# Expert blocks: tokens split once into high and low parts, permutation and gates as two single-pass products each

## The chip, the cores and the metric

The kernel runs on one core of a Trainium2 chip. The metric is the device time of one execution in microseconds (us). One execution was taken by the hardware profiler; every row shown below is from that one. The engines are called PE (matrix products), PEld (loads of the stationary operand of a product, which overlap PE), DVE, ACT and POOL (elementwise work) and SP (here it issues the transfers of weights).

## The reference

Two layers are computed for 384 tokens of width 1024 (128 context tokens, 256 latent ones), the first with attention, the second with a scan. Each layer ends with a grouped mixture of experts, and only that part is touched:

```python
def grouped_moe(h, router_w, router_bias, w_in, w_out, sh_in, sh_out):
    t = h.reshape(-1, d)
    scores = jax.nn.sigmoid((t @ router_w).astype(jnp.float32))
    ...
    gates = jnp.sum(jax.nn.one_hot(idx, N_EXPERTS, dtype=jnp.float32) * w[..., None], axis=1)
    hid = swiglu(jnp.einsum('td,edf->tef', t, w_in))
    routed = jnp.einsum('tef,efd->td', hid * gates[..., None].astype(hid.dtype), w_out)
    shared = swiglu(t @ sh_in) @ sh_out
    return (routed + shared).reshape(bsz, n, d)
```

There are 16 experts in 4 groups; a token goes to two experts of one group, so at most one group of four experts has gates other than zero for it.

## The kernel before

Activations lie feature by token (`hn`, 8 chunks of 128 features by 384 tokens). Products that need more than single-pass accuracy come in two kinds. One is plain fp32, one call for one product. The other, `mm3`, splits both operands into a high part of type F32R (a product of two F32R operands takes a single pass) and a low part, and makes three single-pass products, high by high, high by low and low by high (lines 1836 to 1838).

The mixture of experts is the function `moe`, written once for each engine, and runs once in each layer:

1. The router's product (line 2062), then six transposes of `hn` into token-by-feature order, jobs tok0 to tok5 (line 2077). ACT copies each from its PSUM bank to `h_tok` (line 894), and that copy gives the bank back. Six banks rotate over all jobs, so tok5 needs the bank that tok0 had, and the shared expert's first job the bank of tok1.
2. DVE finds group, experts and gates (`top_experts`, some 40 small steps, each waiting for the one before). After `member_ready` PE counts the tokens of each group (rank, line 2111), and DVE works out where each token goes (`find_places`): `place` (line 1536) is a matrix of zeros and ones, 384 tokens by 7 blocks of 128 slots. Tokens of one group are put into blocks of their own; there are 3 to 6 blocks, and in this execution 5 in the first layer and 4 in the second.
3. Meanwhile PE does the shared expert (`shared_up`, line 2088; its second matrix, line 2128).
4. `permute` (line 2097) gathers one block's tokens: for each of 8 chunks and 3 token tiles one plain product with 128x128 of `h_tok` stationary and 128 columns of `place` moving. It comes in two halves of 12 products. Block 0 is gathered ahead of the loop, both halves in a row.
5. The gates of all blocks (line 2135): 21 plain products with 128x128 of `place` stationary and 4 columns of `rt` moving.
6. The loop over blocks. Four experts each: `up` (32 products by 512 columns through `mm3`), a transpose of the hidden values (line 2162), `down` (line 2166). Weights come in 24 pieces of 512 KB to a block, through six slots: SP loads a piece into `raw`, ACT makes its high part `whi` (line 912), DVE or POOL its low part `wlo` (lines 1567, 610), PE uses them. The two halves of the next block's `permute` stand in the order between the third and fourth transposes and `down(2)` and `down(3)`, which wait for DVE's `ht_lo` (line 1579). ACT and DVE split the gathered block into `blk_hi` and `blk_lo` (lines 904, 905, 1558).
7. `place` is transposed (line 2201), and the blocks' results go back to the tokens (line 2212).

The order on each engine is written out by hand; engines wait for each other by semaphores.

Of the kernel before, what the change touches and what calls it, by code (L numbers as in the profile page):

```python
# [23 lines left out]
F32 = mybir.dt.float32  # L24
F32R = mybir.dt.float32r
ALU = mybir.AluOpType
# [3 lines left out]
P = 128  # L30
D = 1024
# [238 lines left out]
def build(nc, inp, out):  # L270
    ctx = ExitStack()
    with ctx:
# [80 lines left out]
        place = mm.put("place", [TILES, BLOCK_COLS * P])  # L353
# [3 lines left out]
        h_tok = mm.put("h_tok", [TILES, D])  # L357
# [4 lines left out]
        gates = mm.put("gates", [BLOCK_COLS, PER_GRP])  # L362
        gate_now = mm.put("gate_now", [PER_GRP])
        score_rows = mm.put("score_rows", [NTOK])
        sg = mm.put("sg", [2, NTOK])
        p2 = mm.put("p2", [2, NTOK])
# [51 lines left out]
        def sem(name):  # L418
            return ctx.enter_context(nc.semaphore(name))
# [19 lines left out]
        member_ready, groups_ready, place_ready, kmoe_in, gain_ready = (  # L439
            sem("member_ready"), sem("groups_ready"), sem("place_ready"), sem("kmoe_in"), sem("gain_ready"))  # L440
# [86 lines left out]
        def bk(job):  # L527
            return bank[BANK_OF[job][0]]

        def took(ins, job):  # L530
            ins.then_inc(bank_taken[BANK_OF[job][0]], 1)
# [137 lines left out]
        def _(act):  # L669
# [206 lines left out]
            def moe(layer, x_jobs):  # L876
# [10 lines left out]
                for i in range(2 * TILES):  # L887
                    if i == 2:
                        n = JOB[f"scores{layer}"]
                        finished(act, n)  # L890
                        took(act.copy(rt[:, 0, :], bk(n)[:, 0:TILES * NEXP]), n)
                    n = JOB[f"tok{layer}_{i}"]
                    finished(act, n)
                    took(act.copy(h_tok[:, i // 2, (i % 2) * 512:(i % 2 + 1) * 512], bk(n)[:, :]), n)
# [280 lines left out]
        def _(dve):  # L1175
# [258 lines left out]

            def top_experts(layer):
# [4 lines left out]
                def col(i, w=E):  # L1440
                    return rt[:, i, 0:w]
# [34 lines left out]
                dve.tensor_scalar(col(11, G), col(6, G), 1.0, None, ALU.mult).then_inc(member_ready, 1)  # L1476

# [3 lines left out]
                for one in (8, 9):  # L1481
# [7 lines left out]
                    if one == 8:  # L1489
# [8 lines left out]
                                     rt[:, 10, :].rearrange("p (t g i) -> p t i g", g=NGRP, i=PER_GRP), AX.X, ALU.add))  # L1498

# [39 lines left out]
            def moe(layer):  # L1539
# [3 lines left out]
                for kc in range(KC):  # L1543
                    scaled_x(kc)
                top_experts(layer)
# [280 lines left out]
        def _(pe):  # L1826
# [229 lines left out]
            def moe(layer):  # L2056
# [36 lines left out]
                def permute(it, half, base=PERM_BANK):  # L2093

                    for kc in range(4 * half, 4 * half + 4):
                        for t in range(TILES):
                            ins = pe.matmul(bank[base + kc // 4][:, (kc % 4) * P:(kc % 4 + 1) * P],  # L2097
                                            h_tok[:, t, kc * P:(kc + 1) * P], place[:, t, bass.ds(it * P, P)],
                                            start=t == 0, stop=t == TILES - 1)
                    ins.then_inc(ls.perm_done, 1)  # L2100
# [32 lines left out]
                for b_ in range(BLOCK_COLS):  # L2133
                    for t in range(TILES):
                        ins = pe.matmul(dst[:, b_ * PER_GRP:(b_ + 1) * PER_GRP], place[:, t, b_ * P:(b_ + 1) * P],
                                        rt[:, 12, t * PER_GRP:(t + 1) * PER_GRP], start=t == 0, stop=t == TILES - 1)
# [61 lines left out]
                for b_ in range(MAX_BLOCKS):  # L2198
                    dst = opened(JOB[f"back{layer}_{b_}"])
                    for t in range(TILES):  # L2200
                        ins = pe.transpose(dst[:, t * P:(t + 1) * P], place[:, t, b_ * P:(b_ + 1) * P], k("ident"))
                    ins.then_inc(jobs_done, 1)
# [356 lines left out]
```

## Time and profile before

| | us |
|---|---|
| median of 3 runs | 1413.44 |
| lowest and highest run | 1408.8 and 1415.91 |
| the profiled execution, own time | 1415.64 |
| its span, first to last instruction | 1413.8 |
| PE busy, share of the span | 1186.6, 84% |
| DVE busy, share of the span | 861.0, 61% |
| ACT busy, POOL busy | 621.8, 512.3 |
| mean granted TensorE clock | 0.923 |

The profiled execution lies 2.2 us above the median, within the spread of the three runs; 1.8 us of its time lie outside the span. Busy shares are averages over stages with different limits, so the stages of the mixture of experts are read one by one in the rows further down: the routing stage (380 to 441 us in the first layer, 1158 to 1222 us in the second) and the block loop (442 to 655 us and 1225 to 1392 us). A matmul's own duration holds its way through the array; how fast a row of them goes is read from their starts.

### The profile page before, as it was taken

To read this page: it belongs to the slowest core of one execution; us is meant where nothing else is said; L and a number is where in the kernel's file an instruction comes from. 1 tells how busy PE (TensorE), PEld (TensorE's weight loads), DVE (VectorE), ACT (ScalarE), POOL (GpSimd) and SP (SyncE) were. 2 spreads that over 40 slices of the span, in tenths; PEclk is the share of its full clock that TensorE was granted. 3 is DMA by queue.
4 is the path that set the end of the run, shared out by engine and by line. 5 is a ranking of instruction groups with operands and counts; after the bars stand their busy time and mean duration, and the time that the engine had idled before them with its cause. 6 is when DMAs were issued, how large, how long until landed. Compare 5 with 4: busy or idle time off the path is not lost.

```text
span 1413.8 us, 17268 instructions
## 1 busy us (share of the span) xinstructions
PE 1186.6 (84%) x6208; PEld 937.1 (66%) x6208; DVE 861.0 (61%) x1269; ACT 621.8 (44%) x984; POOL 512.3 (36%) x224
## 2 busy tenths in 40 slices
PE   4799877777899999999789999554548789999998
PEld 1685442336767777788589999443436776777778
DVE  2546883355336878883477700999995123588883
ACT  2524113263325657765464433423334313466661
POOL 0513120003004445554035553556553600355550
PEclk9799799996999999999999999677779999899999
DMA  8644138870225888884123333434420302589871
GB/s 336 233 149 148 60 109 334 353 264 31 91 102 179 287 299 300 290 293 170 63 81 119 118 127 106 131 115 125 119 68 1 149 0 81 173 296 324 303 265 45
DMA packets 80031, 241.68 MB, mean 171 GB/s; under 512 B 6624, under 2 KB 38880, under 8 KB 67168
## 3 DMA queue, kind: packets, MB, share of 16 engines
q1 hardware_dynamic: 46512, 218.65, 42.7%
q10 hardware_dynamic: 33456, 22.20, 5.6%
q8 instruction: 38, 0.62, 0.2%
q14 instruction: 25, 0.20, 0.0%
HBM read 236.36 MB, written 4.46 MB: 170 GB/s over the span
## 4 chain that ended last, share of the span: by engine, by line
PE 51%; DVE 19%; issue 11%; DMA 7%; POOL 5%; ACT 5%; SPq 0%; ACTq 0%; DVEq 0%; POOLq 0%
PE bank L1836 10%; PE bank L1838 9%; PE bank L1837 9%; DMA raw<-stream 4%; DVE wlo L1567 3%; PE bank L2088 3%; DVE seg L1773 3%; DMA raw<-experts 3%; POOL wlo L610 3%; PE bank L1854 3%; PE bank L2097 2%; DVE seg L1799 2%; PE bank L2212 2%; POOL wlo L593 2%; PE bank L1898 2%
## 5 line engine op out<-in xcount | busy, mean ns | idle before, releaser
L593 POOL TENSOR_TENSOR wlo<-raw,whi 128x2048 fp32r<-128x2048 f32 x42 | 192.1, 4579 | 379.4 <-ACT whi L676 379.4
L1567 DVE TENSOR_TENSOR wlo<-raw,whi 128x1024 fp32r<-128x1024 f32 x144 | 258.3, 1817 | 33.3 <-ACT whi L912 32.0
L912 ACT CAST whi<-raw 128x1024 fp32r<-128x1024 f32 x216 | 225.2, 1051 | 95.6 <-PE bank L1838 51.1
L610 POOL TENSOR_TENSOR wlo<-raw,whi 128x1024 fp32r<-128x1024 f32 x72 | 199.7, 2774 | 173.6 <-ACT whi L912 173.6
L1836 PE MATMUL bank<-hhi,whi 128*128 128x384 f32 (+1 forms) x504 | 176.4, 350 | 17.4 <-DVE hlo L1233 7.9
L1837 PE MATMUL bank<-hlo,whi 128*128 128x384 f32 (+1 forms) x504 | 173.8, 345 | 0.0
L1838 PE MATMUL bank<-hhi,wlo 128*128 128x384 f32 (+1 forms) x504 | 173.4, 344 | 0.0
L1836 PE MATMUL bank<-whi,blk_hi 128*128 128x512 f32 x288 | 116.6, 405 | 2.6 <-issue 1.4
L1836 PEld LDWEIGHTS bank<-hhi,whi 128*128 128x128 f32 (+1 forms) x504 | 96.4, 191 | 27.5 <-POOL wlo L593 11.9
L1837 PE MATMUL bank<-wlo,blk_hi 128*128 128x512 f32 x288 | 114.1, 396 | 0.0
L1838 PE MATMUL bank<-whi,blk_lo 128*128 128x512 f32 x288 | 114.1, 396 | 0.0
L1431 DVE SCALAR_TENSOR_TENSOR x<-bank,mod,x 128x128 f32<-128x128 f32 x96 | 34.5, 413 | 122.5 <-PE bank L1838 90.9
L676 ACT CAST whi<-raw 128x2048 fp32r<-128x2048 f32 x42 | 79.3, 1905 | 57.3 <-PE bank L1838 34.4
L1838 PEld LDWEIGHTS bank<-hhi,wlo 128*128 128x128 f32 (+1 forms) x504 | 96.4, 191 | 0.5
L1837 PEld LDWEIGHTS bank<-hlo,whi 128*128 128x128 f32 (+1 forms) x504 | 96.6, 192 | 0.1
L1854 PE MATMUL bank<-raw,silc 128*32 128x512 f32 x384 | 57.2, 695 | 37.6 <-DMA raw<-stream 25.0
L2330 PE MATMUL bank<-seg,xdt 128*64 128x128 f32 x384 | 38.5, 338 | 53.6 <-DVE seg L1799 43.7
L1836 PE MATMUL bank<-whi,ht_hi 128*128 128x512 f32 x144 | 59.9, 416 | 17.6 <-DVE ht_lo L1579 17.6
L2330 PEld LDWEIGHTS bank<-seg,xdt 128*64 128x64 f32 x384 | 29.2, 173 | 62.1 <-issue 62.1
L1773 DVE TENSOR_SCALAR seg<-rowb,dts 128x128 f32<-128x128 f32 x192 | 69.4, 432 | 0.1
L1127 ACT ACTIVATE seg<-seg 128x512 f32<-128x512 f32 x48 | 29.6, 626 | 82.7 <-DVE seg L1773 82.7
L1836 PEld LDWEIGHTS bank<-whi,blk_hi 128*128 128x128 f32 x288 | 55.2, 192 | 15.2 <-issue 4.2
(332 smaller groups left out, 2344.2 us busy)
## 6 DMA issues: line engine op xcount, KB each, us to landing
raw<-experts SPq DMA_DIRECT2D x216, 512.0 KB, 4.7
raw<-stream SPq DMA_DIRECT2D x93, 1024.0 KB, 6.2
rowb<-acs_rows ACTq DMA_DIRECT2D x48, 256.0 KB, 4.6
shared<-shared SPq DMA_DIRECT2D x6, 1024.0 KB, 7.9
s<-s0T ACTq DMA_DIRECT2D x8, 256.0 KB, 4.9
new_s<-pf ACTq DMA_DIRECT2D x16, 128.0 KB, 2.1
x<-xT ACTq DMA_DIRECT2D x1, 1536.0 KB, 13.6
yT<-x SPq DMA_DIRECT2D x8, 192.0 KB, 1.9
```

Source lines behind the costliest of these rows:

```text
L593: pool.tensor_tensor(wlo[:, q % SPL, :], raw[:, pos % RAW, :], whi[:, q % SPL, :].bitcast(F32), ALU.subtract).then_inc(lo_done, 1)
L610: pool.tensor_tensor(unit(wlo, j), unit(raw, j), unit(whi, j).bitcast(F32), ALU.subtract).then_inc(ls.e_lo[j % SLOTS], 1)
L676: act.copy(whi[:, q % SPL, :], raw[:, pos % RAW, :]).then_inc(hi_done, 1)
L912: act.copy(unit(whi, j), unit(raw, j)).then_inc(ls.e_hi, 1)
L1567: dve.tensor_tensor(unit(wlo, j), unit(raw, j), unit(whi, j).bitcast(F32), ALU.subtract).then_inc(ls.e_lo[j % SLOTS], 1)
L1773: ins = dve.tensor_scalar(seg[:, n % 2, dr, i * P:(i + 1) * P], rowb[:, n % 2, dr, i * P:(i + 1) * P], acs3[:, t, h:h + 1], 0.0, ALU.subtr ...
L1836: pe.matmul(dst, whi_, xhi_, start=first, stop=False)
L1837: pe.matmul(dst, whi_, xlo_, start=False, stop=False)
L1838: return pe.matmul(dst, wlo_, xhi_, start=False, stop=last)
L1854: ins = pe.matmul(bank[MOD_BANK][32 * grp:32 * grp + 32, :], silc[:, m_, :], raw[:, pos % RAW, grp * 512:(grp + 1) * 512], start=m_ == 0, ...
L2088: ins = pe.matmul(dst, w[:, c, kc, :], hn[:, kc, :], start=kc == 0, stop=kc == KC - 1)
L2330: ins = pe.matmul(dst[64 * p_:64 * p_ + 64, c * P:(c + 1) * P], lhs, rhs, start=j < 2, stop=j >= len(terms) - 2, skip_group_check=True)
```

## The change

`h_tok` is replaced by `tok_hi` and `tok_lo`, both F32R, `place` becomes F32R (zeros and ones, so it loses nothing), and each plain product of the permutation becomes two single-pass products, of `tok_hi` and of `tok_lo`, into the same sum. The gates are split in the same way into `gsplit`, and each plain product of the gates becomes two.

ACT's six copies to `h_tok` become six casts to `tok_hi`, in the same places. DVE gets six subtractions to `tok_lo` in each layer: two ahead of `top_experts`, four behind `member_ready`; these now give the banks of tok0 to tok5 back. DVE also gets two small instructions behind the gates, for `gsplit`. Some tiles are laid out anew. POOL and SP have the same rows as before.

```diff
@@ act, moe
-                    took(act.copy(h_tok[:, i // 2, (i % 2) * 512:(i % 2 + 1) * 512], bk(n)[:, :]), n)
+                    act.copy(tok_hi[:, i // 2, (i % 2) * 512:(i % 2 + 1) * 512], bk(n)[:, :]).then_inc(tok_hi_ready, 1)
@@ dve
+            def token_low(layer, i):
+
+                n = JOB[f"tok{layer}_{i}"]
+                w = slice((i % 2) * 512, (i % 2 + 1) * 512)
+                dve.wait_ge(tok_hi_ready, 2 * TILES * layer + i + 1)
+                took(dve.tensor_tensor(tok_lo[:, i // 2, w], bk(n)[:, :], tok_hi[:, i // 2, w].bitcast(F32),
+                                       ALU.subtract), n)
...
                 dve.tensor_scalar(col(11, G), col(6, G), 1.0, None, ALU.mult).then_inc(member_ready, 1)
+                for i in range(2, 2 * TILES):
+                    token_low(layer, i)
...
+                g12 = rt[:, 12, 0:TILES * PER_GRP]
+                do(dve.tensor_copy(gsplit[:, 0, :], g12))
+                do(dve.tensor_tensor(gsplit[:, 1, :], g12, gsplit[:, 0, :].bitcast(F32), ALU.subtract))
...
+                token_low(layer, 0)
+                token_low(layer, 1)
                 top_experts(layer)
@@ pe, permute
-                            ins = pe.matmul(bank[base + kc // 4][:, (kc % 4) * P:(kc % 4 + 1) * P],
-                                            h_tok[:, t, kc * P:(kc + 1) * P], place[:, t, bass.ds(it * P, P)],
-                                            start=t == 0, stop=t == TILES - 1)
+                            for part in (tok_hi, tok_lo):
+                                ins = pe.matmul(bank[base + kc // 4][:, (kc % 4) * P:(kc % 4 + 1) * P],
+                                                part[:, t, kc * P:(kc + 1) * P], place[:, t, bass.ds(it * P, P)],
+                                                start=t == 0 and part is tok_hi,
+                                                stop=t == TILES - 1 and part is tok_lo)
@@ pe, gates
-                        ins = pe.matmul(dst[:, b_ * PER_GRP:(b_ + 1) * PER_GRP], place[:, t, b_ * P:(b_ + 1) * P],
-                                        rt[:, 12, t * PER_GRP:(t + 1) * PER_GRP], start=t == 0, stop=t == TILES - 1)
+                        for i in range(2):
+                            ins = pe.matmul(dst[:, b_ * PER_GRP:(b_ + 1) * PER_GRP], place[:, t, b_ * P:(b_ + 1) * P],
+                                            gsplit[:, i, t * PER_GRP:(t + 1) * PER_GRP],
+                                            start=t == 0 and i == 0, stop=t == TILES - 1 and i == 1)
```

Two places show it in the engines' order. A row of these lists is one call of the kernel; one plain product is one row there and two instructions on the chip, as the trace's counts show (24 plain products of a block's permutation are 48 instructions).

PE in the first layer, from the shared expert to the permutation of block 0, before:

```order
L2088 MATMUL bank<-hn,shared 128x384 [waits bank_taken1,shared_in1]
L2088 MATMUL bank<-hn,shared 128x384 x7
L2088 MATMUL bank<-hn,shared 128x384 [waits bank_taken2]
L2088 MATMUL bank<-hn,shared 128x384 x7
L2097 MATMUL bank<-place,h_tok 128x128 [waits bank_taken3,place_ready]
L2097 MATMUL bank<-place,h_tok 128x128 x23
L2128 MATMUL bank<-p_105,shared 128x384 [waits shared_in2,bank_taken3,bank_taken2,bank_taken5]
```

and after:

```order
L2107 MATMUL bank<-hn,shared 128x384 [waits bank_taken1,shared_in1]
L2107 MATMUL bank<-hn,shared 128x384 x7
L2107 MATMUL bank<-hn,shared 128x384 [waits bank_taken2]
L2107 MATMUL bank<-hn,shared 128x384 x7
L2117 MATMUL bank<-place,tok_hi 128x128 [waits bank_taken3,place_ready]
L2117 MATMUL bank<-place,tok_lo 128x128
...
L2149 MATMUL bank<-p_107,shared 128x384 [waits shared_in2,bank_taken3,bank_taken2,bank_taken5]
```

The 24 calls of one permutation become 48, alternating between the two parts, at the same place and behind the same waits; in the loop, too, a half stands where it stood.

DVE in the first layer, from the scaled activations to `member_ready` (line 1476 before) and on, before:

```order
L1218 TENSOR_TENSOR hn<-x,rstd 128x384 x7
L1454 TENSOR_TENSOR rt<-rt,vec 128x48 [waits bank_taken5]
...
L1475 TENSOR_TENSOR rt<-rt 128x12 [waits dve_step]
L1476 TENSOR_SCALAR rt<-rt 128x12 [waits dve_step]
L1478 TENSOR_TENSOR rt<-rt 128x48
...
L1497 TENSOR_REDUCE rt<-rt 128x12 [waits dve_step]
L1508 COPY nums<-bank 128x16 [waits jobs_done,dve_step]
```

and after:

```order
L1222 TENSOR_TENSOR hn<-x,rstd 128x384 x7
L1444 TENSOR_TENSOR tok_lo<-bank,tok_hi 128x512 [waits tok_hi_ready] x2
L1466 TENSOR_TENSOR rt<-rt,vec 128x48 [waits bank_taken5]
...
L1487 TENSOR_TENSOR rt<-rt 128x12 [waits dve_step]
L1488 TENSOR_SCALAR rt<-rt 128x12 [waits dve_step]
L1444 TENSOR_TENSOR tok_lo<-bank,tok_hi 128x512 [waits tok_hi_ready] x4
L1492 TENSOR_TENSOR rt<-rt 128x48
...
L1511 TENSOR_REDUCE rt<-rt 128x12 [waits dve_step]
L1514 CAST gsplit<-rt 128x12 [waits dve_step]
L1515 TENSOR_TENSOR gsplit<-rt,gsplit 128x12 [waits dve_step]
L1525 COPY nums<-bank 128x16 [waits jobs_done,dve_step]
```

Two subtractions stand ahead of the routing, four behind `member_ready`, and the two instructions for `gsplit` ahead of the copy that waits for PE's rank.

## Rows read from the trace of the kernel before

**Rows 1.** PE groups by line and shape: count | busy us, mean ns | idle before.

```profile
L2097 PE MATMUL bank<-place,h_tok 128*128 x432 | 51.2, 275 | 0.0
...
L2135 PE MATMUL bank<-rt,place 128*128 128x4 f32 x84 | 11.6, 275 | 0.0
...
L2097 PE MATMUL bank<-place,h_tok 128*128 128x128 f32 x96 | 11.0, 275 | 0.0
```

**Rows 2.** The chain that ended last, 380 to 700 us: start us, us, what.

```profile
419.48 5.36 PE bank L2097 x48
...
435.16 5.22 PE bank L2135 x42
...
525.04 2.68 PE bank L2097 x24
```

**Rows 3.** The block loops as stretches: busy time of each engine, clock, transfers.

```profile
441.80:655.00 213.20, 202.56 (x1000) 167.47 (x1001) 167.99 (x139) 139.14 (x172) 106.31 (x39) 0.98 0.83 290
1224.60:1392.00 167.40, 160.47 (x812) 133.60 (x811) 132.06 (x111) 111.32 (x140) 84.52 (x30) 0.99 0.76 268
```

**Rows 4.** PE in order of time, block 0's permutation: start us, us, instruction, count.

```profile
419.32 5.52 PE L2097 MATMUL bank<-place,h_tok 128*128 128x128 f32 x48
424.67 0.81 PE L2128 MATMUL bank<-p,shared 128*128 128x384 f32 x2
```

**Rows 5.** PEld in order of time: loads for products of 4 columns (rank).

```profile
408.21 0.75 PEld L2111 LDWEIGHTS bank<-rt,kon 128*128 128x128 f32 x6
408.88 0.30 PEld L2088 LDWEIGHTS bank<-hn,shared 128*128 128x128 f32 x2
```

**Rows 6.** PEld in order of time: first single-pass loads behind an idle stretch.

```profile
477.06 0.19 PEld L1836 LDWEIGHTS bank<-whi,ht_hi 128*128 128x128 f32 x1 [0.49 <-DVE ht_lo L1579]
477.17 0.19 PEld L1837 LDWEIGHTS bank<-wlo,ht_hi 128*128 128x128 f32 x1
477.40 0.19 PEld L1838 LDWEIGHTS bank<-whi,ht_lo 128*128 128x128 f32 x1
```

**Rows 7.** PE in order of time: single-pass products, 512 columns, then 384.

```profile
446.94 0.40 PE L1838 MATMUL bank<-whi,blk_lo 128*128 128x512 f32 x1
...
454.44 0.39 PE L1838 MATMUL bank<-whi,blk_lo 128*128 128x512 f32 x1
...
659.20 0.34 PE L2212 MATMUL bank<-back,yhi_e 128*128 128x384 f32 x1
...
669.08 0.34 PE L2212 MATMUL bank<-back,ylo_e 128*128 128x384 f32 x1
```

**Rows 8.** Stretches around rank, permutation, gates, block 0: the third last number is the clock.

```profile
407.00:408.90 1.90, 1.90 (x19) 1.90 (x18) 0.00 (x0) 0.00 (x0) 0.00 (x0) 1.00 0.00 0
...
435.00:437.90 2.90, 2.90 (x28) 2.90 (x26) 2.70 (x4) 0.00 (x0) 2.68 (x2) 1.00 0.00 0
437.90:440.40 2.50, 2.46 (x17) 2.37 (x16) 0.31 (x1) 0.00 (x0) 2.50 (x2) 0.71 0.00 0
441.70:445.80 4.10, 4.03 (x10) 3.17 (x11) 1.04 (x1) 1.04 (x1) 1.02 (x1) 0.50 0.97 328
```

**Rows 9.** DVE in order of time, first layer's routing: start, us, instruction, [idle before].

```profile
395.45 0.21 DVE L1454 TENSOR_TENSOR rt<-rt,vec 128x48 f32<-128x48 f32 x1 [7.87 <-ACT rt L891]
...
402.76 0.24 DVE L1497 TENSOR_REDUCE rt<-rt 128x12 f32<-128x48 f32 x1
409.16 0.17 DVE L1508 COPY nums<-bank 128x16 f32<-128x16 f32 x1 [6.16 <-PE bank L2111]
...
412.60 1.88 DVE L1536 TENSOR_SCALAR place<-kmoe,nums 128x896 f32<-128x896 f32 x3
...
425.98 1.29 DVE L1558 TENSOR_TENSOR blk_lo<-bank,blk_hi 128x512 fp32r<-128x512 f32 x2 [5.84 <-ACT blk_hi L905]
```

**Rows 10.** ACT's first two token copies and PE's first shared product, in order of time.

```profile
394.25 1.07 ACT L894 COPY h_tok<-bank 128x512 f32<-128x512 f32 x2
...
396.66 10.49 PE L2088 MATMUL bank<-hn,shared 128*128 128x384 f32 x32
```

More of the change, by code:

```diff
@@ L352, in build @@
         kmoe = mm.put("kmoe", [KMOE_W])
-        place = mm.put("place", [TILES, BLOCK_COLS * P])
+        place = mm.put("place", [TILES, BLOCK_COLS * P], F32R)
         back = mm.put("back", [MAX_BLOCKS, NTOK], F32R)
         msq = Map(mm.at).put("msq", [SQS, NTOK])
-        h_tok = mm.put("h_tok", [TILES, D])
+        tok_hi = mm.put("tok_hi", [TILES, D], F32R)
+        tok_lo = mm.put("tok_lo", [TILES, D], F32R)
         blk_hi = mm.put("blk_hi", [KC, P], F32R)
@@ L362, in build @@
         gates = mm.put("gates", [BLOCK_COLS, PER_GRP])
+        gsplit = mm.put("gsplit", [2, TILES * PER_GRP], F32R)
         gate_now = mm.put("gate_now", [PER_GRP])
         score_rows = mm.put("score_rows", [NTOK])
-        sg = mm.put("sg", [2, NTOK])
-        p2 = mm.put("p2", [2, NTOK])
+        ml = Map(mm.at)
+        sg = ml.put("sg", [2, NTOK])
+        p2 = ml.put("p2", [2, NTOK])
         sg_e = mm.put("sg_e", [2, D_EXP])
@@ L438, in build @@
             sem("o_done"), sem("o_taken"), sem("osq_ready"), sem("o_normed"), sem("ohi_ready"), sem("olo_ready"))
-        member_ready, groups_ready, place_ready, kmoe_in, gain_ready = (
-            sem("member_ready"), sem("groups_ready"), sem("place_ready"), sem("kmoe_in"), sem("gain_ready"))
+        member_ready, groups_ready, place_ready, kmoe_in, gain_ready, tok_hi_ready, tok_lo_ready = (
+            sem("member_ready"), sem("groups_ready"), sem("place_ready"), sem("kmoe_in"), sem("gain_ready"),
+            sem("tok_hi_ready"), sem("tok_lo_ready"))
         class LoopSems:
@@ L2200, in moe @@
                     for t in range(TILES):
-                        ins = pe.transpose(dst[:, t * P:(t + 1) * P], place[:, t, b_ * P:(b_ + 1) * P], k("ident"))
+                        ins = pe.transpose(dst[:, t * P:(t + 1) * P], place[:, t, b_ * P:(b_ + 1) * P].bitcast(F32), k("ident"))
                     ins.then_inc(jobs_done, 1)
```

## The prediction

> **What bounds the kernel now.** I read the PE groups first, for the size of what is replaced, then the chain of waits for where it lies, then the starts of single instructions for what limits their pace. The permutation is 528 instructions (432 and 96) and the gates 84 [rows 1]. The 528 are 264 plain products, that is 22 halves of 12: two halves ahead of the loop in each layer, and two in each of the 5 and 4 blocks. The reader is to see in the chain that a first permutation stands on the path whole, 5.36 us, and the gates, 5.22 us; in the first layer's loop 7 of the 10 halves stand there, 2.68 us each, of which one row is shown [rows 2]. In the loop PE is busy for 202.6 of 213.2 us and 160.5 of 167.4 us; DVE, next, for 168.0 and 132.1 [rows 3]. So PE sets the loop's pace, and time saved in PE would mostly be saved in the end.
>
> How fast does the permutation go? 48 instructions start from 419.32 to 424.67 us: 5.35 / 48 = **111.5 ns** each [rows 4]. Two things could set that pace, the streaming of columns or the load of a new stationary operand, which every instruction needs. Single-pass products show the streaming: 33 of 512 columns in 454.44 - 446.94 = 7.50 us are 227.3 ns each, 57 of 384 columns in 9.88 us are 173.3 ns [rows 7]; 128 columns more cost 54.0 ns in one pass. A plain instruction of 128 columns, half of a plain product of four passes, thus streams for about 108 ns. The load: rank's products move only 4 columns, so next to nothing streams, and still six loads take 408.88 - 408.21 = 0.67 us, **111.7 ns** each [rows 5], at the full granted clock of 2.4 GHz [rows 8]. So the old permutation sits on both limits at once: about 108 ns of columns and about 111 ns of loads. The change halves the first alone.
>
> **The change part by part.**
>
> *Permutation.* A half was 12 plain products, 24 instructions with 24 loads; it becomes 24 single-pass products, 24 instructions with 24 loads, of 128x128 each. The stationary operand is `tok_hi` or `tok_lo`, another one each time, so no load falls away. What does a load of the single-pass type cost? Where PE had stood idle, two such loads start 110 ns apart (477.06 and 477.17), the second with no product ahead to hold it up; the third, held behind 512 columns, starts 230 ns later [rows 6]. That is the pace of the plain loads. So I take 111.5 ns for an instruction afterwards too: 24 x 111.5 = 2.68 us for a half, as now, and a gain of 0. The bounds: if loads didn't matter, the 384-column row less two steps of 54 ns, 173.3 - 108 = 65 ns, 1.1 us less for a half. If the single-pass kind adds its own excess to the load, at most the 173.3 ns less three steps of 54 ns, 11 ns, 0.3 us more for a half, 6 us for all 22. I am nearest to the middle value because both rows of loads say 110 to 112 ns and neither depends on columns.
>
> The Trainium skill, page "TensorE: Matmul & The Clock Gate", section "Back-to-back issue gap", gives about 81 ns for each pair of a load and a product of 128 columns in a sustained stream. By it an instruction would go from 111.5 to 81 ns; the loads here, at 111.7 ns with almost nothing to stream, speak against it for operands of 4 bytes. This is weighed below as a rival.
>
> *Gates.* 21 plain products of 4 columns, 42 instructions, become 42 single-pass products of 4 columns. Their 42 loads of `place` took 5.22 us [rows 2], 124 ns each, of which the later ones ran at a falling clock (0.71) [rows 8]. Loads set this pace, and there are as many of them: gain 0.
>
> *DVE's six subtractions and two small steps, in each layer.* The nearest row is the same form: `blk_lo` of 128x512 from a bank, two in 1.29 us, 0.65 us each [rows 9]. Two of them ahead of the routing: ACT's first two copies run from 394.25 us for 1.07 us [rows 10], so the subtractions would end near 395.5 and 396.2 us, and the routing, which began at 395.45 us, begins 0.7 us later. Four behind `member_ready` are 2.6 us, and the two steps for `gsplit`, priced like the last small step (0.24 us each), 0.5 us. So DVE is done at about 403.0 + 3.8 = 406.8 us, and then waits for PE's rank, which came at 409.16 us after 6.16 us of waiting [rows 9]. The cover is that wait, and it holds with 2.4 us to spare; `place`, ready at 414.5 us, stays where it was, 4.8 us ahead of the permutation at 419.32 [rows 4, 9]. If both covers were gone, it would cost 3.8 us in each layer. Rank needs `member_ready`, which lies inside the routing and so, even 0.7 us later, well ahead of rank's start near 407 us [rows 8].
>
> *Banks.* They are given back by DVE, not ACT. The shared expert's first product waits for the bank of tok1, which is now free near 396.2 us instead of 395.3; it began at 396.66 [rows 10]. The last transposes need the bank of tok0, free near 395.5. Both have about half a microsecond or more to spare; if that is gone, it costs some tenths of a microsecond, once in a layer. ACT's casts of the same size replace its copies, and the wait of `find_places`, POOL and SP are untouched. Nothing inside the loop but the permutation is changed.
>
> *Sum.* 1415.64 us (the profiled execution, 2.2 us above the median of the runs) plus 0 for permutation, gates and DVE: no change. Against the median I forecast **1413 us**, and 1407 to 1420 us if this reading is right, 7 us below and above being the runs' own spread and the 6 us bound.
>
> **The rivals.**
>
> *Loads are not the limit for single-pass operands.* For it: no row of before has a single-pass product under 384 columns, so that loads of this type follow each other at 110 ns for long is read from pairs behind a stall. Against it: both pairs of rows above. At 65 ns a half is shorter by 24 x 46 = 1.1 us; four first halves give 4.5 us, and 18 halves in the loop 20 us, of which 7 in 10 stood on the path, 14 us: 1413 - 18 = **1395 us**. Past that the waits for `ht_lo` behind a permutation would grow, and 7 in 10 is generous. By the skill's 81 ns it would be 24 x 30 = 0.7 us for a half, 2.9 + 9.2 = 12 us in sum, 1401 us; the trace doesn't bear that figure out. The same page, section "Weight-path perf modes", has loads go faster unless the type is FP32, which would help here if F32R counted as another type; loads of both types take 190 ns from start to end here [rows 6], so the trace speaks against that too.
>
> *The clock falls (slower).* PE then streams columns for only about 54 of 111 ns in a permutation, where before it streamed almost without a break. The granted clock fell from 2.4 GHz to 1.2 GHz behind the gates, where PE had done nothing but loads with 4 columns each: 1.00, then 0.71, then 0.50 while block 0 had already begun, with 512-column products [rows 8]. There 10 of them fill 4.1 us, 0.41 us each instead of 0.23, so that stretch lost about 2 us. If each of the 11 permutations drew one like it, that is 22 us: **1435 us**; if the permutation's own second half, 2.7 us, also took double, 52 us. It decides if a permutation with gaps between its columns is treated as that stretch of gates was. Against it: with rank, 1.9 us of loads with 4 columns each, the clock stayed at 1.00 [rows 8], and a half is 2.7 us with full products on both sides.
>
> *A narrow single-pass product is no single pass (slower; the change doesn't do what it says).* Nothing below 384 columns was seen. If a product of 128 columns took what a whole plain product takes, 223 ns, a half would be 2.7 us longer, 22 halves 59 us: **1472 us**. Against it: pace by columns is even between 384 and 512.
>
> **How the numbers follow.** No change on the path: 0.79. Loads not the limit: 0.11. Clock: 0.07. No single pass: 0.03. A measurement of this kernel can tell about 0.5%, 7 us, from no change. Of the first case some 0.73 falls within 0.5%, 0.03 below and 0.03 above; with a little of the first rival and of the clock's mild end, within 0.5% gets 0.75, faster 0.13, slower 0.12. The range of 1401 to 1423 us holds the first case whole; its low end is the first rival with two thirds of its gain (12 of 18 us), its high end the second with half of its 22 us. That leaves out 0.18.
>
> **What would show it.** Right: 528 permutation instructions of one pass that start 110 to 112 ns apart, a half of 2.7 us, gates of 42 instructions in 5.2 us, DVE's six subtractions of 0.65 us a layer with a wait for rank still behind them, granted clock in the loop near 0.98. Wrong: starts 65 to 80 ns apart (first rival); granted clock of 0.5 in or behind a permutation (second); starts over 200 ns apart at full clock (third); `place` later than PE's arrival at the first permutation (the cover).

## The result, and the profile after

The changed kernel takes 1417.19 us (median of 20 runs, 1408.97 to 1423.48); the kernel before takes 1411.14 us (20 runs, 1402.87 to 1420.28). The ratio is 1.0044, with a 95% interval from 1.0026 to 1.0062: slower by some 6 us. No change was forecast. The profiled execution took 1416.49 us, its span 1414.7 us.

First the replaced work itself. PE's groups by line and shape of the kernel after (count | busy us, mean ns | idle before) answer to [rows 1]:

```profile
L2117 PE MATMUL bank<-place,tok_hi 128*128 x216 | 50.0, 278 | 0.0
L2117 PE MATMUL bank<-place,tok_lo 128*128 x216 | 49.4, 276 | 0.0
L2157 PE MATMUL bank<-gsplit,place 128*128 128x4 f32 x84 | 12.4, 284 | 0.0
L2117 PE MATMUL bank<-place,tok_hi 128*128 128x128 f32 x48 | 11.3, 285 | 0.0
L2117 PE MATMUL bank<-place,tok_lo 128*128 128x128 f32 x48 | 10.8, 274 | 0.0
```

Again 528 and 84 instructions. Their mean duration is not half of before, but the same (275 ns before, 274 to 285 ns now). The busy times of the two permutation groups can't be added and set against before, since an instruction's record begins while the one ahead still runs, and `tok_hi` and `tok_lo` alternate. How far apart they start tells more. PE in order of time, block 0's permutation of the kernel after (start us, us, instruction, count; [rows 4] before):

```profile
415.52 0.28 PE L2117 MATMUL bank<-place,tok_lo 128*128 128x128 f32 x1
415.63 0.28 PE L2117 MATMUL bank<-place,tok_hi 128*128 128x128 f32 x1
...
420.65 0.28 PE L2117 MATMUL bank<-place,tok_lo 128*128 128x128 f32 x1
```

From 415.52 to 420.65 us there are 46 steps: 5.13 / 46 = 111.5 ns each, to the tenth of a nanosecond what it was before. One pass fewer, and no gain. From 415.16 us, the first permutation, to 430.84 us, the gates, it is 15.68 us, as before (419.32 to 435.00 us). The first record of a row is left out of the count: a row's first single-pass product is recorded 0.03 us behind the product ahead of it and its second 0.35 us later, where for plain products it is 0.32 and 0.11 us. In the loop, from the product ahead of a half to the one behind it (second halves, at the full clock), it is 2.74 us against 2.71: 0.03 us more, some 0.6 us over all 18 halves.

The gates keep their pace too. PE in order of time, from their second product on at the full clock, in the kernel before:

```profile
435.02 3.16 PE L2135 MATMUL bank<-rt,place 128*128 128x4 f32 x27
```

and in the kernel after:

```profile
431.17 3.15 PE L2157 MATMUL bank<-gsplit,place 128*128 128x4 f32 x27
```

Without the last one's own 0.25 us, 26 steps take 2.91 us before and 2.90 us after: 112 ns each in both.

DVE, which got the six subtractions, in order of time, first layer's routing of the kernel after ([rows 9] before):

```profile
391.00 1.29 DVE L1444 TENSOR_TENSOR tok_lo<-bank,tok_hi 128x512 fp32r<-128x512 f32 x2 [6.96 <-ACT tok_hi L898]
...
395.00 2.48 DVE L1444 TENSOR_TENSOR tok_lo<-bank,tok_hi 128x512 fp32r<-128x512 f32 x4
...
402.38 0.17 DVE L1515 TENSOR_TENSOR gsplit<-rt,gsplit 128x12 fp32r<-128x12 f32 x1
405.30 0.18 DVE L1525 COPY nums<-bank 128x16 f32<-128x16 f32 x1 [2.75 <-PE bank L2132]
```

The subtractions take 0.65 and 0.62 us each, and DVE still waits 2.75 us for PE's rank behind them, where it waited 6.16 us before. They cost nothing.

So where is the loss? These are the block loops as stretches (us, then busy time of PE, PEld, DVE, ACT and POOL with counts, granted clock, share and GB/s of transfers), first layer and second, of the kernel after:

```profile
438.20:655.40 217.20, 206.91 (x1000) 172.06 (x1001) 160.12 (x139) 138.91 (x172) 108.33 (x39) 0.95 0.80 285
1220.80:1391.00 170.20, 164.97 (x801) 137.57 (x802) 123.07 (x110) 109.70 (x136) 88.00 (x31) 0.95 0.77 270
```

and the second layer's loop of the kernel before on the same bounds, from the first product of block 0 to the first transpose of `place` ([rows 3] begins that loop 3 us later):

```profile
1221.60:1390.10 168.50, 161.57 (x801) 134.15 (x802) 131.48 (x110) 109.75 (x136) 84.81 (x31) 0.98 0.77 273
```

The first loop is 4.0 us longer (213.20 in [rows 3], now 217.20), the second 1.7 us (168.50, now 170.20). From the gates to the loop it is 0.6 and 0.3 us more, from the router to the permutation 0.6 and 0.3 us less; 0.3 us of each is only the earlier record of a row's first single-pass product. That is about 5.7 us in the expert blocks. The two profiled spans differ by 0.9 us only, because other parts of the execution happened to be 4.8 us shorter: 3.5 us of it lie ahead of the first layer's router, where nothing was changed. In the loops PE's busy time rose by 4.4 and 3.4 us with the same number of instructions, its idle time did not rise (10.6 to 10.3 us, 6.9 to 5.2 us), and the granted clock fell from 0.98 to 0.95. PE does the same instructions, some of them at 1.2 instead of 2.4 GHz.

Where it falls is seen at the first permutation inside the loop. PE in order of time, kernel after:

```profile
467.94 0.30 PE L2117 MATMUL bank<-place,tok_hi 128*128 x1
...
470.54 0.28 PE L2117 MATMUL bank<-place,tok_lo 128*128 x1
472.46 0.80 PE L1855 MATMUL bank<-whi,ht_hi 128*128 128x512 f32 x1 [1.64 <-DVE ht_lo L1598]
473.05 0.63 PE L1856 MATMUL bank<-wlo,ht_hi 128*128 128x512 f32 x1
473.47 0.63 PE L1857 MATMUL bank<-whi,ht_lo 128*128 128x512 f32 x1
```

and the stretches around it, of the same kernel (columns as above, the clock third from the end):

```profile
465.00:467.90 2.90, 2.90 (x14) 2.30 (x13) 2.90 (x2) 2.20 (x3) 1.53 (x1) 1.00 0.90 339
467.90:470.70 2.80, 2.80 (x27) 2.77 (x25) 1.93 (x3) 1.96 (x4) 2.54 (x1) 1.00 1.01 354
470.70:472.40 1.70, 0.12 (x2) 0.00 (x0) 1.70 (x3) 0.49 (x1) 0.28 (x1) 0.97 1.01 410
472.40:475.80 3.40, 3.34 (x8) 2.70 (x9) 1.13 (x2) 0.32 (x1) 0.00 (x0) 0.51 1.01 328
475.80:479.00 3.20, 3.20 (x26) 2.92 (x25) 0.82 (x2) 2.05 (x3) 2.40 (x1) 1.00 0.65 261
```

Full products at 1.00, then the first half of the permutation at 1.00, then 1.64 us of waiting for `ht_lo`, and the next eight 512-column products run at 0.51, starting 0.43 us apart instead of 0.23. In the loops of the kernel before one such low stretch stands, 520.9 to 524.3 us (the one behind the gates, which reaches into the start of each loop in both kernels, is not counted here); after there are six, 472.3 to 475.7, 516.7 to 520.1, 557.6 to 564.5, 605.4 to 608.8, 1298.3 to 1301.7 and 1339.3 to 1346.1 us, together 27.3 us. Every one begins within 1.2 us of the end of a wait for `ht_lo` directly behind a half of the permutation.

What does one cost? By whole blocks (from a block's first `up` product to the next one's; the middle blocks of both layers, in all profiles of this study with halves of equal size), 32 blocks without a low stretch take 41.7 us in the mean, 16 blocks with one of 3.4 us take 43.5. So it costs about half its length. The second and third blocks of [rows 3]'s first loop, as two stretches of the kernel before, show one of each kind:

```profile
485.66:530.34 44.68, 41.44 (x201) 34.11 (x201) 35.11 (x30) 29.13 (x36) 21.66 (x8) 0.96 0.82 286
530.34:572.38 42.04, 39.88 (x201) 32.99 (x201) 35.17 (x30) 29.24 (x36) 21.83 (x8) 1.00 0.84 297
```

### The profile page after: what moved, and what is told of

Same layout as the page of the kernel before. It is cut to its first block, busy times and chain, and to the rows that moved or that the text cites. A ratio compares the mean times of both kernels' runs of the same rounds, so it can differ in the third digit from the quotient of the medians.

```text
span 1414.7 us, 17284 instructions
## 1 busy us (share of the span) xinstructions
PE 1191.9 (84%) x6208; PEld 942.3 (67%) x6208; DVE 851.8 (60%) x1285; ACT 621.8 (44%) x984; POOL 517.5 (37%) x224
## 4 chain that ended last, share of the span: by engine, by line
PE 46%; DVE 16%; issue 15%; POOL 11%; DMA 6%; ACT 5%; ACTq 0%; SPq 0%; POOLq 0%; DVEq 0%
PE bank L1855 9%; PE bank L1856 9%; PE bank L1857 9%; POOL wlo L614 8%; DMA raw<-stream 4%; PE bank L2107 3%; DVE seg L1792 3%; DVE seg L1818 2%; PE bank L2235 2%; PE bank L1873 2%; POOL wlo L597 2%; PE bank L1917 2%; PE bank L2353 2%; PE bank L2117 1%; DMA raw<-experts 1%
## 5 line engine op out<-in xcount | busy, mean ns | idle before, releaser
L614 POOL TENSOR_TENSOR wlo<-raw,whi 128x1024 fp32r<-128x1024 f32 x72 | 205.1, 2850 | 173.4 <-ACT whi L916 173.4
L1586 DVE TENSOR_TENSOR wlo<-raw,whi 128x1024 fp32r<-128x1024 f32 x144 | 241.4, 1701 | 42.2 <-ACT whi L916 42.0
L1855 PE MATMUL bank<-whi,ht_hi 128*128 128x512 f32 x144 | 63.0, 438 | 15.5 <-DVE ht_lo L1598 15.5
```

Of the source, the lines that this page charges most:

```text
L614: pool.tensor_tensor(unit(wlo, j), unit(raw, j), unit(whi, j).bitcast(F32), ALU.subtract).then_inc(ls.e_lo[j % SLOTS], 1)
L1586: dve.tensor_tensor(unit(wlo, j), unit(raw, j), unit(whi, j).bitcast(F32), ALU.subtract).then_inc(ls.e_lo[j % SLOTS], 1)
L1855: pe.matmul(dst, whi_, xhi_, start=first, stop=False)
```

## The experiments

The **theory** after the result: the permutation keeps its pace, but fills only half of it with columns; behind a first half PE then waits for `ht_lo`, and the two together bring the clock down for the `down` products that follow. The **rivals**: the loss sits in the gates or in DVE's new steps; it is the change of type and not the gaps; it is the wait alone, which the kernel before has too.

**Which part of the change?** Each part alone: e1_gates_only puts the split gates into the kernel before, e2_permute_only takes them out of the kernel after.

```diff
# e1_gates_only, against before
+                        for i in range(2):
+                            ins = pe.matmul(dst[:, b_ * PER_GRP:(b_ + 1) * PER_GRP], place[:, t, b_ * P:(b_ + 1) * P],
+                                            gsplit[:, i, t * PER_GRP:(t + 1) * PER_GRP],
# e2_permute_only, against after
-                        for i in range(2):
-                                            gsplit[:, i, t * PER_GRP:(t + 1) * PER_GRP],
+                        ins = pe.matmul(dst[:, b_ * PER_GRP:(b_ + 1) * PER_GRP], place[:, t, b_ * P:(b_ + 1) * P].bitcast(F32),
+                                        rt[:, 12, t * PER_GRP:(t + 1) * PER_GRP], start=t == 0, stop=t == TILES - 1)
```

> The gates alone are split, on the kernel before; the permutation stays plain. Clock theory (single-pass permutations stream columns for half of their time, the clock falls where a wait follows them, and the loops lose what the changed kernel lost, some 5.6 us): ratio to before 1.000 within 0.002, loops near 213 and 168 us, at most one low stretch of the clock in them. Rival (gates, place of another type or the two steps for gsplit make the loss): 1.004.

> The permutation alone is changed, with its six subtractions; the gates stay plain products. Clock theory: as the changed kernel, 1.004 (1.002 to 1.006), several low stretches of the clock in the loops, 15 to 30 us of them in sum. Rival (the gates make the loss): 1.000.

Measured: gates alone 1.0003 (0.9978 to 1.0027), permutation alone 1.0057 (1.0029 to 1.0085). The whole loss that can be measured comes with the permutation and the six subtractions, which e2 keeps; e10, further down, has the subtractions too, and no loss. In its profile e1 has one low stretch in the loops, e2 four.

**Does it depend on how full the pass is?** e3_wide lets three chunks of four move 256 columns (the additional 128 are written into the columns of the chunk before, whose own products come later and start its sum anew), so that they fill their instruction as the plain ones did; e8_wide_first_half does so in the first halves alone; e4_narrow goes the other way and moves 32 columns in five of a sum's six products.

```diff
# e3_wide (e8_wide_first_half adds "and half == 0" to wide)
-                    for kc in range(4 * half, 4 * half + 4):
+                    for kc in range(4 * half + 3, 4 * half - 1, -1):
+                        wide = P if base == PERM_BANK and kc % 4 else 0
+                                ins = pe.matmul(bank[base + kc // 4][:, (kc % 4) * P - wide:(kc % 4 + 1) * P],
+                                                place[:, t, bass.ds(it * P - wide, P + wide)],
# e4_narrow
+                                w = P if base != PERM_BANK or (t == 0 and part is tok_hi) else P // 4
+                                                part[:, t, kc * P:(kc + 1) * P], place[:, t, bass.ds(it * P, w)],
```

> As the changed kernel, but in the loop three of four chunks' products move 256 columns of place instead of 128 (the extra 128 go to a neighbour chunk's columns, which are then started anew, so the result is the same). The pace stays that of the loads, 111 ns, and columns fill nearly all of it. Clock theory: the low stretches go from the loops (at most one or two, under 7 us), loops near 213 and 168 us, ratio to before 1.000 within 0.002, against 1.004 for the changed kernel. Rival (anything else of the change, such as DVE's work, the tiles' new places, the type): it stays at 1.004.

> The changed kernel with the 256-column products in the loop's first half of each permutation alone. All six low stretches in the changed kernel's loops begin within 1.2 us of a wait of 1.6 to 2.6 us for ht_lo that follows a first half. Theory (half-filled columns and that wait together bring the clock down): most of the loss is back, 0.999 to 1.003. Rival (every permutation counts alike): half of it, 1.002 to 1.004; or none.

> As the changed kernel, but in the loop only the first product of each sum moves 128 columns, the other five move 32 (three quarters of the gathered tokens' slots are left incomplete, so part of the computation is left out; instructions, loads and waits are the same). The pace stays 111 ns. Clock theory: still fewer columns, so more low stretches, over 27 us of them in the loops, and slower than the changed kernel: 1.006 to 1.015. Rival: as the changed kernel, 1.004, or faster.

Measured: e3 1.0012 (0.9988 to 1.0036), e8 0.9994 (0.9971 to 1.0016), e4 1.0154 (1.0120 to 1.0189). Streaming more columns makes the kernel quicker, streaming fewer makes it slower, with the number of instructions unchanged. Against e2, e3 is quicker by 0.0045, about 0.0037 more or less, although its wide products start 120 ns apart and a half takes 2.88 us instead of 2.74. The loops of e4_narrow as stretches:

```profile
438.80:657.50 218.70, 210.22 (x1000) 174.65 (x1001) 161.62 (x139) 138.91 (x172) 107.71 (x39) 0.94 0.81 283
1225.10:1405.10 180.00, 171.87 (x801) 142.21 (x802) 130.45 (x110) 109.52 (x136) 83.09 (x31) 0.92 0.74 255
```

PE's busy time is 7.7 and 10.3 us above before with as many instructions, at 0.94 and 0.92, and 13 low stretches stand in them, some 48 us together, now also behind second halves, where PE doesn't wait: with so few columns the clock fell without a wait too. A miss: e3 was to have at most one or two low stretches, and its profile has three, e8's too. So wide products don't spare the clock always. PE in order of time in e3_wide, a wait that did no harm:

```profile
521.11 0.28 PE L2118 MATMUL bank<-place,tok_lo 128*128 x1
523.03 0.50 PE L1855 MATMUL bank<-whi,ht_hi 128*128 128x512 f32 x1 [1.64 <-DVE ht_lo L1598]
523.37 0.39 PE L1856 MATMUL bank<-wlo,ht_hi 128*128 128x512 f32 x1
```

The same 1.64 us as in the kernel after at 472.46 us, and the next product starts 0.34 us later instead of 0.59. The last six products of a half are 128 wide in e3 too, right ahead of the wait; whether that is why some still fall wasn't tried.

**Type, or columns?** Plain products with fewer columns, in the kernel before: e7_plain_narrow moves 32 columns in two of three token tiles (as many column times in a half as the single-pass products of 128), e9_plain_quarter 32 in all.

```diff
# e7_plain_narrow
+                            w = P if base != PERM_BANK or t == 0 else P // 4
# e9_plain_quarter
+                    w = P if base != PERM_BANK else P // 4
```

> The kernel before, plain fp32, but in the loop the products of the second and third token tile move 32 columns instead of 128 (the gathered blocks are left incomplete, so part of the computation is left out). Over three products that is as much column time as the single-pass products of the changed kernel have; the instructions and loads are those of before. Clock theory (columns, not the type, decide): slower than before as the changed kernel is, 1.003 to 1.007, with several low stretches of the clock in the loops. Rival (the F32R type itself, or the six subtractions and the new tiles, cost the time): 1.000.

> The kernel before, plain fp32, with every product of the loop's permutations moving 32 columns instead of 128 (three quarters of each gathered block are not computed, so part of the computation is left out). Instructions and loads are those of before, and the pace stays at 111 ns; the type is untouched. Clock theory (columns decide, not the type): low stretches in the loops as with the single-pass products at 32 columns, 20 to 48 us of them, ratio 1.006 to 1.015. Rival (the type F32R decides): 1.000.

Measured: e7 1.0022 (1.0001 to 1.0043), between the two theories, with no low stretch in its profile's loops: inconclusive (the profile is of its quickest run, and only two waits of over 1 us stand behind a half in it). e9 1.0029 (1.0004 to 1.0055), under what was expected of it, but with six low stretches of some 24 us in its profile. So the type is not needed for the clock to fall: plain products with few columns do it too. But e9 cost less than e4 with its 1.0154. The two aren't quite the same test: by the prediction's streaming times (54 ns for 128 columns in one pass, 108 ns in a plain instruction) an estimated 27 ns of columns fill an instruction of e9, and 20 ns in the mean one of e4. Whether that or the type makes the difference stays open.

**Gates between other products.** The clock also falls behind the gates, in both kernels [rows 8]. e5_gates_between (on before) deals the gates out between the shared expert's last products, so that no 5 us of narrow products stand in a row; e6_wide_between does that on top of e3.

```diff
+                    if i == 4:
+                        gdst = opened(JOB[f"gate{layer}"])
+                    for b_ in range(2 * (i - 4), min(2 * (i - 4) + 2, BLOCK_COLS)) if i >= 4 else ():
+                        for t in range(TILES):
+                            ins = pe.matmul(gdst[:, b_ * PER_GRP:(b_ + 1) * PER_GRP], place[:, t, b_ * P:(b_ + 1) * P],
```

> The kernel before, with the gates' 42 instructions no longer in one stretch behind the shared expert but behind its last four jobs, two blocks each. If a stretch with few columns brings the clock down, the fall behind the gates (at the start of both loops) goes or comes later, and the gates' pace stays at 111 ns: up to 3 us less in each layer, ratio 0.995 to 0.999. Rival (the start of the loop is bound by something else, such as the weights, or the fall only moves): 1.000.

> The changed kernel with 256-column products in the loop's permutations and the gates between the shared expert's last jobs. If both remedies work and add up: 0.996 to 1.000. Rival (the gates' place doesn't matter): 1.001, as with 256 columns alone.

Measured: e5 1.0008 (0.9987 to 1.0030), e6 1.0019 (0.9994 to 1.0043): no gain. PE in order of time in e5_gates_between, the end of the gates and the loop's first products:

```profile
437.85 0.73 PE L2134 MATMUL bank<-rt,place 128*128 128x4 f32 x6
440.05 0.49 PE L1836 MATMUL bank<-whi,blk_hi 128*128 128x512 f32 x1 [1.47 <-issue]
440.38 0.39 PE L1837 MATMUL bank<-wlo,blk_hi 128*128 128x512 f32 x1
440.60 0.51 PE L1838 MATMUL bank<-whi,blk_lo 128*128 128x512 f32 x1
440.91 0.63 PE L1836 MATMUL bank<-whi,blk_hi 128*128 128x512 f32 x1
```

The loop begins at the full clock, which then falls at the third product, behind a pause of 1.47 us: in the first layer the fall was moved by a microsecond, and the low stretch halved (6.8 us before, 3.4 us now). In the second layer it is gone, and still nothing is gained. That layer's first block as a stretch (columns as for the loops), in the kernel before:

```profile
1221.57:1265.55 43.98, 42.41 (x200) 35.12 (x201) 32.58 (x27) 27.37 (x33) 20.42 (x8) 0.93 0.82 296
```

and in e5_gates_between:

```profile
1215.53:1259.52 43.99, 40.84 (x200) 32.85 (x201) 36.13 (x29) 27.22 (x33) 25.39 (x10) 1.00 0.82 303
```

PE is busy for 1.57 us less, at the full clock, and the block takes as long: PE waits for the difference. So both times are those of the rivals (1.000 and 1.001), and this row fits the first of them, that something other than PE's pace sets the start of the loop.

**Taking the wait away.** The sharpest test leaves the products as they are and covers the wait instead. Six chunks of eight go into the first half and two into the second, so that DVE has ended `ht_lo`, or nearly so, when PE comes to it (the halves become 36 and 12 instructions long); once on the kernel after, once on the kernel before.

```diff
# e10_six_two (on after), e11_plain_six_two (on before)
-                    for kc in range(4 * half, 4 * half + 4):
+                    for kc in (range(6), range(6, KC))[half]:
```

> The changed kernel with six of the eight chunks of a permutation ahead of down(2) and two ahead of down(3), instead of four and four. In all traces so far PE waits 1 to 2.6 us for ht_lo behind most first halves, and never behind a second. Theory (half-filled columns and that wait together bring the clock down): the wait shrinks by up to 1.3 us a block, the falls go from the loops, and with both the kernel is faster than the changed one by 6 to 12 us: 0.993 to 1.000 of before. Rival (the wait moves to down(3), or the weights set the pace): as the changed kernel, 1.004.

> The kernel before with the same six and two chunks; the permutation stays plain. If the wait behind the first half is PE's own loss, up to 1.3 us a block comes back: 0.992 to 0.998. If it only moves, 1.000. Against the run with single-pass products it tells what the type still costs when no wait follows it.

Measured: e10 0.9935 (0.9913 to 0.9957), 1400.87 us; e11 0.9932 (0.9907 to 0.9958), 1400.53 us. Both beat both kernels, and with the wait covered no difference can be told between the two kinds of products. PE in order of time in e10_six_two, behind the 36 products of a first half:

```profile
509.04 0.28 PE L2117 MATMUL bank<-place,tok_lo 128*128 x1
509.36 0.50 PE L1855 MATMUL bank<-whi,ht_hi 128*128 128x512 f32 x1
509.69 0.39 PE L1856 MATMUL bank<-wlo,ht_hi 128*128 128x512 f32 x1
```

No wait, and full pace, behind 4 us of half-filled products in a row (505.10 to 509.04 us). The longest wait behind any of its first halves is 0.42 us. The loops as stretches, e10_six_two:

```profile
435.10:636.90 201.80, 200.01 (x1000) 166.59 (x1001) 158.41 (x139) 139.03 (x172) 109.64 (x39) 0.99 0.86 305
1203.70:1366.60 162.90, 161.48 (x800) 134.45 (x801) 126.69 (x110) 110.27 (x136) 84.09 (x31) 0.98 0.80 282
```

and e11_plain_six_two:

```profile
439.10:644.10 205.00, 200.41 (x1000) 166.51 (x1001) 161.22 (x139) 139.71 (x172) 105.54 (x39) 0.99 0.86 302
1208.70:1371.40 162.70, 161.25 (x800) 134.26 (x801) 126.19 (x110) 110.35 (x136) 84.89 (x31) 0.98 0.80 282
```

PE's idle time in the loops goes from 10.6 and 6.9 us [rows 3, and the second loop above] to 1.8 and 1.4 us (e10), 4.6 and 1.5 us (e11), and no low stretch stands in them. In the profiled executions this is worth more than in the medians, since they were among the quickest of their kernels; the medians, about 10 us under before, decide.

**All waits together.** Counted over the loops of all profiles: waits of over 1 us directly behind a half of the permutation, and how many of them the clock fell at (within 1.5 us of the wait's end).

| Products of the permutation | kernels | waits over 1 us | clock fell |
|---|---|---|---|
| plain, 128 columns | before, e1, e5 | 13 | 1 |
| one pass, 128 columns | after, e2 | 14 | 10 |
| one pass, three in four with 256 columns | e3, e6, e8 | 12 | 7 |
| plain, two in three with 32 columns | e7 | 2 | 0 |
| plain, 32 columns | e9 | 6 | 5 |
| one pass, five in six with 32 columns | e4 | 5 | 5 |
| one pass or plain, 6/2 | e10, e11 | 0 | 0 |

The first two rows show the theory. One of the 13, in the kernel before, where the clock stayed (PE in order of time):

```profile
1256.95 0.50 PE L1836 MATMUL bank<-whi,ht_hi 128*128 128x512 f32 x1 [1.56 <-DVE ht_lo L1579]
1257.29 0.39 PE L1837 MATMUL bank<-wlo,ht_hi 128*128 128x512 f32 x1
```

The waits of the second row are somewhat longer (1.3 to 2.6 us against 1.1 to 1.9), but that is not the cause: among waits of 1.4 to 1.8 us alone the clock fell at 0 of 8 in the first row and at 5 of 9 in the second. The third row is nearer to the second than the times are (1.0012, 1.0019 and 0.9994 against 1.0044 and 1.0057); these are one profiled execution each, and how much 256 columns spare the clock stays open.

Can the wait do it alone? Seldom, but it can. In the loops of before, after, e1, e2, e3, e5, e6, e8, e10 and e11, 38 more waits of over 1 us have no half of the permutation directly ahead, and the clock fell at four of them, of 1.8 to 2.25 us (one in e1, two in e6, one in e8). PE in order of time in e1_gates_only, where only full products stand ahead of the wait:

```profile
593.89 0.39 PE L1842 MATMUL bank<-whi,blk_lo 128*128 128x512 f32 x1
596.41 0.50 PE L1840 MATMUL bank<-whi,ht_hi 128*128 128x512 f32 x1 [2.14 <-DVE ht_lo L1583]
597.84 0.63 PE L1842 MATMUL bank<-whi,ht_lo 128*128 128x512 f32 x1
```

## Why the prediction was wrong

Point by point, by its own steps:

*The permutation's pace: right.* 111.5 ns was forecast and 111.5 ns was measured; the load of the stationary operand sets it for both kinds of product. The Trainium skill's 81 ns for a load and a product of 128 columns (page "TensorE: Matmul & The Clock Gate", section "Back-to-back issue gap") doesn't hold here in either kernel, and the rival that rested on a quicker load, 1395 us, or 1401 by that figure, is out. So is the one that feared a narrow single pass would be no single pass, 1472 us.

*The gates: right.* No gain came, as forecast, and the pace is 112 ns before and after. Of the excess that the prediction put into its bounds for the permutation, 0.3 us for a half, 0.03 us appeared.

*DVE's cover: right.* 2.4 us of the wait for rank were to be left, 2.75 us were. The subtractions were priced at 0.65 us and took that.

*The banks: right.* The router's stretch to the first permutation did not grow.

*The clock: this is the step that failed.* The prediction's sum holds nothing for the clock. It had the mechanism as a rival, "The clock falls (slower)", and gave it 0.07. It put it aside because "a half is 2.7 us with full products on both sides", and because the clock stayed at 1.00 over rank's 1.9 us of narrow products [rows 8]. The first is not so: behind most first halves PE does not go on to full products, but waits for `ht_lo`, for 1.1 to 1.9 us behind 5 of 9 in the kernel before and for 1.5 to 2.6 us behind 7 of 9 in the one after, where the clock fell at six of the seven. The prediction knew of these waits, since its first rival has them grow; it counted them for time and not for the clock. Rank was no fitting row, because PE goes on from it without a pause [rows 5]; nor was the row of the gates, where the clock fell amid 5 us of products with 4 columns [rows 8]. No row of before has half-filled products with a wait behind them, and a case without a row should have kept a larger share than 0.07.

*The size of that rival was off too.* 22 us were 11 falls of 2 us. In the profile it is six falls against one, with some 24 us more at the low clock. At half its length each that would be 12 us, but only 5.7 us of longer loops are found, since waits that PE would have had anyway take up a part (its idle time fell by 2.1 us) and low stretches lie partly over waits; 0.6 us of the 5.7 are the halves' slightly slower pace. The Trainium skill, page "TensorE: Matmul & The Clock Gate", section "Terms", reckons the penalty of a throttled stretch at its length times the share of pulses withheld, half here; the 1.8 us that a block with one low stretch of 3.4 us takes longer agree with it, the sum over both loops does not.

*The sum.* 0 was forecast, +6 us (+0.44%) came. 1417.19 us lies within 1401 to 1423 us only because the high end was put at half of this rival's mis-sized 22 us; that is luck. The chance of slower should have been far above 0.12.

What the rows show and what they don't: that half-filled products followed by a wait go with the fall is shown by the two kernels, by e2, and by e10 and e11, which leave the products as they are and take the wait away. That it is the share of columns, and not another property of these products, is borne out by the times of e3, e4 and e8 and not settled: e3, e6 and e8 still have 7 falls at 12 waits, and e7 and e9 do not decide it.

## What to carry to other kernels

Before halving the passes of a product, look at what sets its pace: where 128-column products with a new stationary operand each start as far apart as loads with 4 columns do, a pass saved saves no time, it only leaves the array half empty. Then look at what follows: half-filled products that run straight into a wait of over 1 us can bring TensorE's clock down for the full products behind it, so price a wait by what stands before it also. The wait was the better target all along: giving the first gap six of eight chunks instead of four took some 10 us off the kernel before, and brought the changed kernel to the same time, with one changed line.

## What was unexpected of the hardware

36 half-filled products in a row, 4 us, leave the clock at 2.4 GHz as long as full products follow within 0.4 us (e10); 24 of them with a wait of over 1 us behind them brought it down 10 times in 14. Behind full products a wait of some 2 us can do it too, but seldom does (4 of 38 waits of over 1 us). Against the kernel before, single-pass products with 256 columns in the loop cost nothing that can be told (e3 0.1% more, e8 0.1% less), with 128 columns 0.4% and with 32 columns 1.5%, though they start 112 ns apart in the median with 32 columns as with 128, and 120 ns with 256; in plain fp32 the same 32 columns cost 0.3%.
